# Second block: the early gates' products, one or two at a time between the steps of the scans

## The reference, cut to what matters

```python
proj = x @ w_in
y_a = rwkv7_mixer(proj[..., :OFF_MOBA], ...)          # 8 heads of 64, a recurrence over the tokens
y_b = moba_attention(heads(q), heads(k), heads(v))
y_c = s5_mixer(...)                                   # ends in zg = y @ glu_w + glu_b
gates = sigmoid(proj[..., OFF_GATE:] + gate_b).reshape(B, L, 3, D_MODEL)
merged = (gates[..., 0, :] * (y_a @ w_up_rwkv)
          + gates[..., 1, :] * (y_b @ w_up_moba)
          + gates[..., 2, :] * (y_c @ w_up_ssm))
return merged @ w_out
```

## Time and profile before

| | |
|---|---|
| median of three runs | 1942.84 us |
| the profiled execution | 1936.89 us, of which the span 1935.1 us |
| TensorE busy | 1781.0 us, 92% of the span |
| VectorE, ScalarE, GpSimd busy | 519.9, 251.2, 159.6 us |
| mean granted TensorE clock | 0.981 of full speed |
| read from memory | 494.99 MB |
| the woven scans and gates | 1461.9 to 1601.3 us of the span |

### The profile page before, as it was taken

One profiled execution on the slowest core, in us unless ns is written; L12 is line 12 of the kernel. 1 busy time (PEld: TensorE's weight loads), 2 busy tenths in 40 slices (PEclk: granted clock), 3 DMA queues, 4 the chain that ended last, 5 costly groups with the idle time before them and its releaser, 6 DMA issues.

```text
span 1935.1 us, 52713 instructions
## 1 busy us (share of the span) xinstructions
PE 1781.0 (92%) x24496; PEld 1401.6 (72%) x24496; DVE 519.9 (27%) x1239; ACT 251.2 (13%) x657; POOL 159.6 (8%) x307
## 2 busy tenths in 40 slices
PE   8999999999988999999999999889989999989775
PEld 7758885567588988988898989777757778653331
DVE  2641000224311111110101010146774443242223
ACT  2320000033101000000000000022232112010000
POOL 0000000100007400000000000055430000000000
PEclk9999999999999999999999999989989999999988
DMA  8224433331397999999999999941301028579996
GB/s 322 98 95 183 170 135 148 138 147 44 123 402 314 369 375 401 385 416 360 395 384 389 388 394 399 403 142 32 110 26 64 35 77 367 201 315 427 427 426 275
DMA packets 62952, 498.30 MB, mean 258 GB/s; under 512 B 7096, under 2 KB 15824, under 8 KB 17104
## 3 DMA queue, kind: packets, MB, share of 16 engines
q1 hardware_dynamic: 52672, 490.11, 63.0%
q10 hardware_dynamic: 10128, 5.97, 1.1%
HBM read 494.99 MB, written 1.05 MB: 256 GB/s over the span
## 4 chain that ended last, share of the span: by engine, by line
PE 75%; DMA 17%; DVE 4%; issue 2%; ACT 1%; ACTq 1%; DVEq 0%; SPq 0%
PE pb L1162 12%; PE pb L806 11%; PE pb L1193 10%; DMA ringbuf<-in_ein 10%; PE pb L815 7%; PE pb L811 4%; PE pb L879 3%; PE pb L1064 3%; DMA ringbuf<-in_e2out 2%; PE pb L1407 2%; PE pb L1384 2%; PE pb L1673 2%; DMA arena<-in_e2in 2%; PE pb L1109 2%; DMA ringbuf<-in_e2in 2%
## 5 line engine op out<-in xcount | busy, mean ns | idle before, releaser
L1162 PE MATMUL pb<-arena,ringbuf 128*64 128x80 f32 x11264 | 421.8, 234 | 27.3 <-issue 10.6
L1162 PEld LDWEIGHTS pb<-arena,ringbuf 128*64 128x64 f32 x11264 | 403.4, 138 | 45.3 <-issue 31.8
L1735 DVE TENSOR_TENSOR arena<-arena,pb 128x160 f32<-128x160 f32 (+3 forms) x130 | 48.0, 369 | 647.5 <-ACT arena L2704 402.3
L1193 PE MATMUL pb<-arena,ringbuf 128*64 128x80 f32 x5632 | 202.7, 233 | 16.9 <-issue 16.5
L1193 PEld LDWEIGHTS pb<-arena,ringbuf 128*64 128x64 f32 x5632 | 197.7, 137 | 22.1 <-issue 21.5
L806 PE MATMUL pb<-XT,ringbuf 128*128 128x256 f32 (+2 forms) x1104 | 201.9, 345 | 0.8 <-ACT XT L2504 0.8
L806 PEld LDWEIGHTS pb<-XT,ringbuf 128*128 128x128 f32 (+1 forms) x1104 | 180.3, 192 | 22.1 <-issue 2.1
L2504 ACT ACTIVATE arena<-pb 128x256 f32<-128x256 f32 (+5 forms) x188 | 72.8, 405 | 541.5 <-PE pb L1193 182.6
L815 PE MATMUL pb<-arena 64*64 64x64 f32 (+4 forms) x664 | 106.1, 322 | 6.0 <-DVE Y L1735 3.5
L815 PEld LDWEIGHTS pb<-arena 64*64 64x64 f32 (+4 forms) x664 | 51.8, 152 | 56.4 <-issue 28.6
L811 PE MATMUL pb<-ringbuf,arena 128*128 128x512 f32 x192 | 83.6, 593 | 2.9 <-DVE arena L1735 1.8
(11 more groups left out here) (391 smaller groups left out, 1799.6 us busy)
## 6 DMA issues: line engine op xcount, KB each, us to landing
ringbuf<-in_ein SPq DMA_DIRECT2D x176, 1024.0 KB, 7.4
ringbuf<-in_eout SPq DMA_DIRECT2D x64, 1408.0 KB, 9.7
arena<-in_e2in SPq DMA_DIRECT2D x13, 2048.0 KB, 26.6
ringbuf<-in_e2in SPq DMA_DIRECT2D x12, 2048.0 KB, 35.9
ringbuf<-in_fin SPq DMA_DIRECT2D x11, 2048.0 KB, 7.6
ringbuf<-in_e2out SPq DMA_DIRECT2D x8, 2048.0 KB, 31.3
ringbuf<-in_wo SPq DMA_DIRECT2D x6, 2048.0 KB, 7.8
arena<-in_e2out SPq DMA_DIRECT2D x6, 2048.0 KB, 34.2
```

What stands on the lines that cost most here:

```text
L1162: ins = pe.matmul(PB[4 + f % 2][h_, t * C1:(t + 1) * C1], w3[:, k, (t % 2) * 128 + h_.start:(t % 2) * 128 + h_.stop], XG[e % 2][:, k, :], ...
L1193: ins = pe.matmul(PB[d % 2][h_, 0:C1], w3[:, f, h_], HT[:, f, :], start=f == 0, stop=f == 21)
L1735: return v.tensor_tensor(o, a, b, op)
```

## The change

In `early_gates` TensorE's generator ended a step behind each of the eight products of a gate. Now it ends one behind every second product, and ScalarE's generator has four steps for a gate in place of eight, with its copy in the fourth. The `yield` behind the eighth product stays.

```diff
                         for j in range(8):
                             ins = pe.matmul(PB[5][:, 0:256], w3[:, j, br * 128:(br + 1) * 128], xT[:, j, :], start=j == 0, stop=j == 7)
-                            if j < 7:
+                            if j in (1, 3, 5):
                                 yield
                         ins.then_inc(*egP.up((d, br)))
                         yield
@@ ScalarE
                     for br in range(3):
-                        for _ in range(7):
+                        for _ in range(3):
                             yield
                         a.wait_ge(*egP.at((d, br)))
                         copy(GT[:, d, br, :], PB[5][:, 0:256]).then_inc(*A.up(egA, (d, br)))
```

## The result

The kernel before took 1942.17 us in the median of its 13 runs beside the changed one (1938.6 to 1944.69), the changed kernel 1951.14 us (13 runs, 1947.5 to 1958.97). The ratio is 1.0049, with a 95% interval of [1.0038, 1.0060]; on 1942.84 us that is +9.5 us. It is slower, outside the range (1938.2 to 1948.8) and against the chance of 0.85 for "same". The profiled execution of the changed kernel took 1949.35 us, its span is 1947.6 us, and the mean granted clock is 0.975 (0.981 before). In all 13 runs of the changed kernel that mean is 0.971 to 0.976; in the 78 runs of the kernel before that stand beside the experiments it is 0.976 to 0.984.

A forecast was written before the change was run, and what follows sets the result against it. TensorE was taken to set the pace in the scans. Terms +19.37 - 4.45 - 14.73 = +0.19 us, plus 1.7 for a clock fall, made +1.9 on 1942.84: 1944.7 us, range 1938.2 to 1948.8.

The forecast's parts named there:

- The first part: Up to the step behind "n2" of the second half: 48 more gate products there, +19.37 us in sum.
- the waits that a second product fills: First part: nine TensorE waits after a single product would hide 2.83 us of the added products.
- the two turns on ScalarE: First part: twice a gate follows another without a scan product between and waits for ScalarE's copy, +1.56 us.
- the 0.96 us before "r": TensorE's wait before "r" would not be hidden, since ScalarE still copies a gate first and "n2" behind it.
- "var" to the glu: 31 products fewer: the glu would start 1.90 us after "var" instead of 16.63, a gain of 14.73 us.
- The sum without a fall: All terms from the first gate product to the merges, without a clock fall: 19.37 - 4.45 - 14.73 = +0.19 us.
- the clock: Idle times from "ys" to the glu would make the granted clock fall, costing 1.7 us in the glu; chance 0.50.
- rival 3: Clock falls behind "s2" and stays low through the bare chain until the glu: +7.1 us, 1949.9 us; chance 0.06.
- "r" to "s1": Products dropped before "u" (three), "an" (one) and "pq" (three) would all be gained, 3.61 us.
- Rival 2: First expert loads issue 10.0 us earlier, so the DMA-bound stretch begins earlier: 1934.7 us; chance 0.06.
- Rival 4: ScalarE's gate copies hold the scan's copies at six of twelve places: +2.9 us, 1947.6 us; chance 0.08.
- Rival 1: No fall of the clock between the scans' bare chain and the glu: +0.2 us, 1943.0 us; chance 0.30.

The follow-up runs named there:

- x8_both: Changed kernel plus seven full-width filler products (results unused): behind "pq", "s1", "s2", two behind "aps", one behind "ys" and "mean"; 1942.36 us, ratio 0.9983 to the kernel before.
- x7_back: Changed kernel plus four full-width filler products (results unused): two behind "aps", one behind "ys", one behind "mean"; 1953.65 us, ratio 1.0054 to the kernel before.
- x9_eights: The 96 gate products without fillers, whole gates of eight where TensorE waits in the weaving's first half, then as x5_fit; 1940.79 us, ratio 0.9984 to the kernel before.
- x3_bare: Kernel before with one gate product per step, but none in the 17 steps from "r" to "var", the remaining 48 behind "var"; 1955.54 us, ratio 1.0052.
- x4_mixed: Against the kernel before: two gate products per step for 32 steps, then one per step for 32, none left behind "var"; 1945.75 us, ratio 1.0014.
- x1_wide: Changed kernel plus eight full-width filler products (results unused) where TensorE waits from "r" to "mean"; 1942.93 us, ratio 0.9998 to the kernel before.
- x2_narrow: As x1_wide, but each filler is eight 64x64 products with 64 columns; 1944.89 us, ratio 1.0003 to the kernel before.
- x5_fit: The same 96 gate products without fillers, laid out by a list where TensorE waits, none left at the end; 1934.28 us, ratio 0.9964 to the kernel before.
- x6_front: Changed kernel plus three full-width filler products (results unused), behind "pq", "s1" and "s2"; 1951.63 us, ratio 1.0045 to the kernel before.

## Why the prediction was wrong

**What it had right.** The first part, 48 products more, was +19.50 against +19.37: the waits that a second product fills, the two turns on ScalarE (0.47 us each), the 0.96 us before "r" that stay. (The change drops eleven groups, 51 to 40, and not ten; no term of the sum hangs on that.) "var" to the glu was -14.63 without the fall (x8_both) against -14.73. The sum without a fall was +1.21 in x8_both against +0.19. So the reading that the gates' work is only paid earlier holds.

**The step that failed** is the clock, as the prediction put it: "a fall of half of the 6.82 us costs 3.41/2 = 1.7 us of TensorE's time in the glu", "since the glu follows without a gap and a busy engine gets its clock back". Its place was wrong (the fall is at "s1", not at the glu), and its length: 27.3 us in place of 3.4, of which the glu's beginning is only the last 5.4. It costs 9.1 us in place of 1.7. In the traces that is 1.21 + 9.12 = +10.33 for the changed kernel. Put into the prediction's sum it gives 0.19 + 9.1 = +9.3, and +9.5 was measured; that these two agree to 0.2 us is partly luck, since the sum without a fall was off by 1 us.

The mechanism was rival 3's, at a chance of 0.06 and +7.1 us. What I held against it was that "'y' and 'ys' are a long run of small products without a wait, in which a low clock has time to return". The changed kernel's fourth and fifth windows, x7_back and x9_eights (98% busy for 20.5 us) show that it doesn't return there; x3_bare's first fall, which ended after 3.4 us among such products, shows that it can. The duration was taken from one fall in the earlier trace rows. It was also misread: the 6.82 us begin at 1436.28, inside the idle 4.51 us that ended at 1438.40, so that behind the idle time the clock was low for 4.70 us. That row tells how long the clock stayed low in another piece of work and nothing of how it would here.

On this the Trainium skill ("TensorE: Matmul & The Clock Gate", section "What's actually happening") says that throttled is the default state and that activity releases it. The traces agree with the two levels. The prediction read its table so that an engine that is never wholly idle for long keeps 2.4 GHz; here the clock fell with no wait above 1.11 us ahead of it. And where that table has a busy engine back at full rate, x9_eights was at 0.50 for 20.5 us, busy for 20.11 of them, for the most part with 64x64 products. In both places the measurement decides.

**The other terms.** "r" to "s1" gave 2.96 us of the forecast 3.61: in the middle of "sa" TensorE idles 0.96 us for nothing that the profile names. x8_both has 0.9 there too, so it isn't the clock; its cause stays open (an idle time of this kind is in x4_mixed too). Rival 2 falls: the first expert loads go out later (1617.01 us), the next wait for TensorE until 1682.81, and the full stretch has its 426 GB/s as before. Rival 4 falls too: up to "r" the only waits in the changed kernel are the two turns, 0.9 us together, and the forecast 0.96 us at "r" itself. Rival 1 (no fall, +0.2 us) is what the kernel comes near to with something in the waits (x8_both).

**What is shown and what open.** Shown: without the fall the same places of the gate products cost nothing that can be measured (x1_wide, x2_narrow, x8_both), so the fall is what makes the kernel slower; it comes from the waits that the products left bare (x3_bare); small products in them are enough (x2_narrow); the front and the back of the stretch both need them (x6_front, x7_back). Open: which quantity decides. x5_fit kept its clock through 9.7 us of small products without waits, x8_both through waits of 0.9 and 1.4 us with a filler beside them, and x9_eights lost it behind waits of 0.69 and 0.33. Busy time alone doesn't explain how long a fall lasts: x3_bare's first was over after 3.4 us, 3.31 of them busy, and that of x9_eights after 20.5, 20.11 busy. Open is also an idle time of 0.67 to 1.93 us without a releaser, which stands once in the middle of small products in every kernel but the one before, x3_bare and x5_fit. It isn't what sets off the fall: x3_bare fell without it, and x2_narrow kept its clock through the longest, 1.93 us.

## What to carry to other kernels

Filler work between the steps of a chain has a second job: it keeps TensorE's clock. Before moving it away, list the waits that stay bare, look at what the granted clock does, and price a fall at the whole stretch up to the next long run of large products (where it ended in the changed kernel, x6_front, x7_back and the second time in x3_bare; in x9_eights and the first time in x3_bare it ended sooner), not at the shortest fall in the trace. And place such work by where the waits are (four products between "mean" and "var", none where the chain runs without a gap) rather than at an even rate; that gave 0.36% here. Ask of the last one whose copy it puts ahead of the scan's.

## What was not expected of the hardware

- The clock stood at 0.50 through 20.5 us in which TensorE was busy for 20.11 us with mostly 64x64 products (x9_eights), and through 27.3 us in x7_back with 24.41 busy. It came back within a whole gate of 128x256 products in x3_bare, 1.9 us after its start, and in the changed kernel 5.4 us after the glu's start. But x3_bare's first fall ended after 3.4 us with 64x64 products alone.
- A fall needs no long wait: it came behind 0.69 and 0.33 us in x9_eights, 7 us after the last gate product. And a longer one needs no fall behind it: x2_narrow kept its clock through 1.93 us.
- Put into each wait, eight 64x64 products (0.68 us) kept the clock as well as one product of 128x256 did (x2_narrow and x1_wide).
